# Three expert passes summed by TensorE alone, from rows gathered as 4 picks x 32 tokens, with 16 row buffers and two ring slots

## What is computed

```python
def peer_ffn(x, w_q, sub_keys, u, v):        # 8 heads, top 16: 128 picks a token
    q = (xt @ w_q).reshape(T, PEER_HEADS, 2, PEER_HALF)
    s = jnp.einsum('thcd,hcnd->thcn', q, sub_keys)
    s1, i1 = lax.top_k(s[:, :, 0], K); s2, i2 = lax.top_k(s[:, :, 1], K)
    ...                                       # best 16 of the 256 sums -> expert_idx, softmax -> gates
    ub = jnp.take(u, eb, axis=0)              # rows of 1024 numbers, 4 KB
    act = gelu(einsum('thkd,td->thk', ub, xb))
    vb = jnp.take(v, eb, axis=0)
    return einsum('thk,thkd->td', gb * act, vb)
```

## Time and profile before

| | |
|---|---|
| median of 3 runs | 2260.46 us (2255.74 to 2270.28) |
| span of the profiled execution | 2259.6 us (the profile records no time outside it) |
| busy in the span | PE 1527.2, DVE 1450.5, POOL 985.0, ACT 323.1 us |
| DMA | 760.62 MB, mean 337 GB/s; of it 536.94 MB by gathers |
| first gather issued | 208.45 us |
| last v row used | 1937.91 us |

### The profile page before, as it was taken

How to read it: one execution, slowest core, us unless ns; L and a number is a source line. 1 busy time by engine, 2 the same in 40 slices (tenths; PEclk the granted TensorE clock), 3 DMA queues, 4 the chain that set the end, 5 groups by cost and what they waited for, 6 DMA issues and landing times. The chain is left out here.

```text
span 2259.6 us, 17114 instructions
## 1 busy us (share of the span) xinstructions
PE 1527.2 (68%) x5282; PEld 879.4 (39%) x5282; DVE 1450.5 (64%) x3168; ACT 323.1 (14%) x778; POOL 985.0 (44%) x1058
## 2 busy tenths in 40 slices
PE   8987600467656539776573897666576656899998
PEld 7446600222225225422341552235252232376453
DVE  1236898779587875678688468786978676444101
ACT  1220100011112111111120111111321000123111
POOL 0102466667665555566455456653446444000000
PEclk9989855688867669987766899778767877899999
DMA  7436999999999999999999999999989999973672
GB/s 260 85 117 245 394 408 409 337 360 370 371 379 403 404 406 358 361 365 367 407 399 405 365 342 368 375 401 386 391 293 403 399 398 399 366 243 130 242 260 93
DMA packets 268005, 760.62 MB, mean 337 GB/s; under 512 B 21295, under 2 KB 46590, under 8 KB 267275
## 3 DMA queue, kind: packets, MB, share of 16 engines
q0 software_dynamic: 147456, 536.94, 61.8%
q1 hardware_dynamic: 120458, 222.60, 27.8%
HBM read 756.84 MB, written 2.62 MB: 336 GB/s over the span
## 5 line engine op out<-in xcount | busy, mean ns | idle before, releaser
L946 POOL DMA_INDIRECT ROWS<-in_peer_u,IDX x512 | 483.3, 944 | 455.5 <-DVE ROWS L991 266.9
L946 POOL DMA_INDIRECT ROWS<-in_peer_v,IDX x512 | 487.8, 953 | 357.2 <-PE bank L292 121.4
L991 DVE SCALAR_TENSOR_TENSOR ROWS<-ROWS,XP 128x1024 f32<-128x1024 f32 x512 | 602.3, 1215 | 23.7 <-issue 12.3
L995 DVE SCALAR_TENSOR_TENSOR XP<-ROWS,GATE,XP 128x1024 f32<-128x1024 f32 x316 | 405.8, 1284 | 155.9 <-DMA ROWS<-in_peer_v,IDX 133.7
L292 PE MATMUL bank<-ROWS,DG 128*128 128x512 f32 x774 | 380.0, 649 | 94.2 <-DMA ROWS<-in_peer_v,IDX 78.5
L292 PE MATMUL bank<-ring,XT 128*128 128x512 f32 (+6 forms) x912 | 392.7, 589 | 62.3 <-DMA ring<-in_ffn_w_up 32.0
L292 PEld LDWEIGHTS bank<-ring,XT 128*128 128x128 f32 x912 | 185.6, 214 | 249.9 <-issue 179.4
L292 PEld LDWEIGHTS bank<-ROWS,DG 128*128 128x128 f32 x774 | 157.5, 209 | 309.8 <-issue 201.8
L292 PE MATMUL bank<-XT,ring 128*128 128x128 f32 (+2 forms) x1504 | 209.4, 301 | 57.1 <-issue 27.4
L292 PEld LDWEIGHTS bank<-XT,ring 128*128 128x128 f32 (+1 forms) x1504 | 198.3, 204 | 71.8 <-issue 35.7
L307 PE MATMUL bank<-CN,X 128*128 128x128 f32 x128 | 27.1, 384 | 184.9 <-issue 90.7
(11 more groups left out here) (408 smaller groups left out, 1461.6 us busy)
## 6 DMA issues: line engine op xcount, KB each, us to landing
ring<-in_peer_w_q SPq DMA_DIRECT2D x16, 2048.0 KB
ring<-in_ple_w_gate SPq DMA_DIRECT2D x9, 2048.0 KB
...
ROWS<-in_peer_u,IDX POOLq DMA_INDIRECT x512
```

The lines of the kernel that those rows point to most:

```text
L946: G.indirect_dma_start(ROWBUF[slot(n, c)][:, :], None, tables[table], bass.IndirectOffsetOnAxis(IDX[:, tt, c:c + 1], axis=0)).then_inc(row ...
L991: V.scalar_tensor_tensor(row, row, 1.0, XP[:, :], ALU.mult, ALU.mult, accum_out=ACTV[:, tt, c:c + 1]).then_inc(row_used, 1)
L995: V.scalar_tensor_tensor(XP[:, :], row, gate, XP[:, :], ALU.mult, ALU.add).then_inc(row_used, 1)
```

## The change

1. **Passes 1, 3 and 5 wholly on TensorE.** `pe_turn_picks` and `dve_turn_picks` turn the table of indices (`IDXF` to `IDXV`), so that a gather brings 4 picks of 32 tokens, partition 32k + i being pick k of token i in the group. The bytes of a gather and their number stay. The gates are turned likewise (`pe_to_quads`, 32 matmuls of 16 columns) and DVE spreads them (`dve_spread`): four instructions of 1024 columns a pass, which make for each gather a stationary operand of 128 rows x 32 columns. PE multiplies a row buffer with it, 2 x 512 columns, and the result goes to 32 of the 128 output partitions: those of q = 0, 1, 2 or 3, by the gather's number in its group of 4. Gathers are taken in pairs: first columns 0 to 511 of both (into accA), then 512 to 1023 of both (accB), and one `pe_used` for the pair. The `DG` buffers and ACT's `act_share` are gone, and DVE has no row of these passes. `dve_sums` reads X and the banks after two rows of the next u pass.
2. **16 row buffers and two ring slots in passes 0 to 5.** The third slot's memory becomes row buffers 12 to 15. From pass 6 on these four are a ring slot again, and 12 row buffers are left. The early loads are placed by a table (`FIRST_SLOT`), some of them in row buffers.
3. **The query weights of layer 0 are loaded once** for both tiles: four loads of 2.10 MB less. Two of the four blocks lie in row buffers 8 to 11 and 12 to 15, so gathers 8 and 12 of pass 0 wait (`kept_read`) until ACT has copied tile 1's queries of those blocks, which are now made first (order 2, 3, 0, 1); the first gather waits for `out_w_read`.
4. DVE does 24 u rows of pass 0 at the end of layer 0's route, ahead of `dve_turn_picks`; the turned picks of later passes are made in `peer_done`.

Its core (lines left out stand as "..."):

```diff
-SLOTS = 12
+SLOTS = 16
 VECTORS = 13
-DIAGS = 4
+GROUP = 4
+QUAD = P // GROUP
...
-RING, SLOT = 3, 4096
+RING, SLOT = 2, 4096
+LATE = SLOTS * D // SLOT - 1
+NARROW = 6
 BANKS = 6
 MORE = SLOTS * D // SLOT
+KEPT_SLOT = {2: 5, 3: 2}
+FIRST_SLOT = {"a_gate": 0, "a_q": 1, "a_k": 3, "a_v0": 4, "a_v1": 0, "a_og0": 1, "a_og1": 3, "keys0": 0, "a_out0": 4, "a_out1": 3,
+              "peer_q0_0": 1, "peer_q0_1": 0, "peer_q0_2": KEPT_SLOT[2], "peer_q0_3": KEPT_SLOT[3]}
...
+            if key in FIRST_SLOT:
+                slot = FIRST_SLOT[key]
+            elif not fewer_rows:
+                slot = (n - len(FIRST_SLOT)) % RING
+            elif not last_gather:
+                slot = (n - fewer_rows[0]) % (RING + 1)
+            else:
+                slot = (n - last_gather[0] + RING + 1) % (RING + MORE)
+            slot_no.append(slot)
+            slot_use.append(slot_no[:n].count(slot))
...
-        enter_cols("peer_q01_", a["peer_w_q"][0], [0, 512, 1024, 1536, 2048])
...
+        fewer_rows.append(len(stream))
...
+                    if n == fewer_rows[0] + RING:
+                        sp.wait_ge(row_used, dve_used(NARROW - 1))
+                        sp.wait_ge(pe_used, tensor_used(NARROW - 1))
+                    elif last_gather[0] <= n < last_gather[0] + MORE - 1:
                         sp.wait_ge(row_used, dve_used(len(passes) - 1))
                         sp.wait_ge(pe_used, tensor_used(len(passes) - 1))
+                    elif before:
+                        sp.wait_ge(*released[before[-1]])
+                    elif n == place["peer_q0_3"]:
+                        sp.wait_ge(S("phase_end"), 3)
...
+        BY_PE = (1, 3, 5)
...
-            return n in SHARED and c % (2 * RUN) >= RUN
+            return n in BY_PE
...
+            if n < NARROW:
+                return (n * PICKS + c) % SLOTS
+            return ((n - NARROW) * PICKS + c) % (SLOTS - SLOT // D)
...
+            return (sum(len(pe_rows_of[m]) for m in range(n)) + (len(pe_rows_of[n]) if k is None else k) + 1) // 2
...
+                if n == 0 and c in (8, 12):
+                    G.wait_ge(S("kept_read"), c // 4 - 1)
+                picks = IDXV if n in BY_PE else IDX
                 G.indirect_dma_start(ROWBUF[slot(n, c)][:, :], None, tables[table],
-                                     bass.IndirectOffsetOnAxis(IDX[:, tt, c:c + 1], axis=0)).then_inc(row_in[slot(n, c)], 16)
+                                     bass.IndirectOffsetOnAxis(picks[:, tt, c:c + 1], axis=0)).then_inc(row_in[slot(n, c)], 16)
...
+                    if n == 0:
+                        pool.wait_ge(S("out_w_read"), 1)
+                    if n in BY_PE:
+                        pool.wait_ge(S("picks_turned"), n // 2 + 1)
...
+        def pe_to_quads(src, name):
+            m = src.shape[1] // GROUP
+            b = job(name)
+            if turn(name) > 1:
+                PE.wait_ge(bank_free(name), turn(name) - 1)
+            for k in range(GROUP):
+                for q in range(GROUP):
+                    last = mul(b[QUAD * k:QUAD * k + QUAD, q:GROUP * m:GROUP], ident[:, QUAD * q:QUAD * q + QUAD],
+                               src[:, k:GROUP * m:GROUP], True, True)
+            last.then_inc(bank_ready(name), 1)
...
+        def dve_turn_picks(l, tt):
+            V.wait_ge(bank_ready("turned"), turn("turned"))
+            V.tensor_copy(IDXV[:, tt, :], result("turned")[:, 0:PICKS]).then_inc(bank_free("turned"), 1)
+            V.wait_ge(bank_free("turned"), turn("turned"))
+            V.sem_inc(S("picks_turned"), 1)
...
+        def spread(tt, x):
+            part = Y[:, tt, :] if x == 2 else later["spread"][:, min(x, 2), :]
+            return part.rearrange("p (j t) -> p j t", t=QUAD)
+        def dve_spread(n, half):
+            tt, name = passes[n][1], f"gv{half}"
+            V.wait_ge(bank_ready(name), turn(name))
+            for x in (2 * half, 2 * half + 1):
+                gates = result(name)[:, QUAD * (x % 2):QUAD * (x % 2) + QUAD]
+                V.tensor_tensor(spread(tt, x), con("spread").unsqueeze(1).broadcast_to([P, QUAD, QUAD]),
+                                gates.unsqueeze(2).broadcast_to([P, QUAD, QUAD]), ALU.mult).then_inc(spread_ready, 1)
+            V.wait_ge(spread_ready, 4 * (n // 2) + 2 * half + 2)
+            V.sem_inc(bank_free(name), 1)
+        def pe_share(n, g0=0, g1=PICKS // GROUP):
+            accs, tt = (result("accA"), result("accB")), passes[n][1]
+            for g in range(g0, g1):
+                first, end = g == 0, g == PICKS // GROUP - 1
+                x, j = divmod(GROUP * g, QUAD)
+                PE.wait_ge(spread_ready, 4 * (n // 2) + x + 1)
+                weights = spread(tt, x)
+                for pair in ((0, 1), (2, 3)):
+                    for q in pair:
+                        PE.wait_ge(*arrived(n, GROUP * g + q))
+                    for q in pair:
+                        to, row = slice(QUAD * q, QUAD * q + QUAD), ROWBUF[slot(n, GROUP * g + q)]
+                        last = mul(accs[0][to, :], weights[:, j + q, :], row[:, 0:512], first, end)
+                    if end and 3 in pair:
+                        last.then_inc(bank_ready("accA"), 1)
+                    for q in pair:
+                        to, row = slice(QUAD * q, QUAD * q + QUAD), ROWBUF[slot(n, GROUP * g + q)]
+                        if end and q == GROUP - 1:
+                            held.clear()
+                            mul(accs[1][to, 0:256], weights[:, j + q, :], row[:, 512:768], False, True).then_inc(bank_ready("accB"), 1)
+                            last = mul(accs[1][to, 256:512], weights[:, j + q, :], row[:, 768:1024], False, True)
+                        else:
+                            last = mul(accs[1][to, :], weights[:, j + q, :], row[:, 512:1024], first, end)
+                    last.then_inc(pe_used, 1)
...
+            A.wait_ge(row_used, dve_used(n))
+            act_copy_x(n + 1)
...
+            if n not in BY_PE:
+                gather_rest()
+                V.scalar_tensor_tensor(Y[:, tt, :], X[:, tt, :], ALPHA, XP[:, :], ALU.mult, ALU.add).then_inc(S("sums_taken"), 1)
+                V.wait_ge(S("sums_taken"), 1)
                 return
+            V.wait_ge(*nth("x_copied", 2))
+            gather_begin(n + 1)
+            gather_some(2)
             V.wait_ge(pe_used, tensor_used(n))
             for i, name in enumerate(("accA", "accB")):
                 V.wait_ge(bank_ready(name), turn(name))
-                y = Y[:, tt, i * 512:(i + 1) * 512]
-                V.tensor_tensor(y, y, result(name)[:, :], ALU.add).then_inc(bank_free(name), 1)
+                s = slice(i * 512, (i + 1) * 512)
+                V.scalar_tensor_tensor(Y[:, tt, s], X[:, tt, s], ALPHA, result(name)[:, :], ALU.mult, ALU.add).then_inc(bank_free(name), 1)
+            gather_some(1)
...
+            to_pe = n + 1 in BY_PE
+            if to_pe:
+                @block.tensor
+                def _(pe):
+                    for i, half in enumerate(halves):
+                        pe.wait_ge(*nth("gate_done", i + 1))
+                        pe_to_quads(GATE[:, tt, half], f"gv{i}")
+                    pe_share_begin(n + 1)
+                    pe_share(n + 1, 0, 2)
...
+                if to_pe:
+                    gather_some(2)
+                    dve_spread(n + 1, 0)
...
-                        pe_share(beside, 6 * e, 6 * e + 6)
+                    if l == 1 and e > 0:
+                        pe_share(beside, 4 * e - 2, 4 * e + 2)
...
-                    for e in range(4):
-                        pe.wait_ge(*landed(f"peer_q{l}{tt}_{e}"))
-                        queries(slot_of(f"peer_q{l}{tt}_{e}"), tt, e)
-                        weight_read(f"peer_q{l}{tt}_{e}", f"q{e}{tt}")
+                    for e in (2, 3, 0, 1):
+                        queries(slot_of(f"peer_q{tag}_{e}"), tt, e)
+                        weight_read(f"peer_q{tag}_{e}", f"q{e}{tt}")
...
+                        A.sem_inc(S("out_w_read"), 1)
...
+                            A.sem_inc(S("kept_read"), 1)
...
+                if l == 0:
+                    gather_some(24)
+                    dve_turn_picks(0, 0)
```

125 lines of the change are left out of this document (53 added, 72 removed).

## The result

The changed kernel took **2327.5 us** (median of 4, 2325.8 to 2329.0) beside 2258.1 for the kernel before: ratio 1.030, interval 1.0272 to 1.0328. The forecast was 2207. But the verdict did not hold everywhere. On five later occasions, each on another chip of known number, the kernel before took 2264 once (chip 6) and 2193 to 2195 four times (chips 0, 12, 11, 4). On chip 12 the changed kernel took 2188, ratio 0.9972 (0.9955 to 0.9989). Two things stay open about these names. The number of the first chip is not on record, so it may be one of the others. And the two slow-issue occasions were the first two in time, and none of the five known chips was met twice: whether the kind belongs to a chip or to a time no run tells.

The account below looks back on a forecast made before the run. DMA engines were taken to bound the 1730 us middle, with v passes losing time to POOL's waits for PE. 2259.6 - 49.4 - 4 = 2206.2, with the median 0.9 above: 2207 us; range 2172 to 2262.

Parts of the forecast that it names:

- Why do they lose?: Passes 1, 3, 5: POOL has next to no reserve, so its waits for PE lose 62.4 us of DMA time.
- the 49.4 us: Passes 1, 3, 5: gain expected from part 1, 62.4 less 13 us of remaining losses; bounds 62 and 41.
- part 2, priced at nothing: Mixer in passes 2 and 4: two slots cost nothing until it is 40 us slower, since PE waited 41.91 us.
- Rival D: V passes as forecast, but first gathers, a mixer over 40 us late or late picks take it back: about 2231; chance 0.12.
- Part 1's price: V rows on PE: overlapping matmuls of different column groups make a row cost 0.87 us, against 1.75 at full clock.
- Rivals B and C: V rows on PE: B, 1.26 us a row, 2236 (0.08) or far slower (0.04); C, 1.75 us, 2412 us (0.16).
- a fall to half clock: PE in v passes: its clock may halve, making a row 1.75 us; the forecast took full clock.
- PE is then far from the bound: Passes 1, 3, 5: v rows need 111 us of PE a pass, 151 us in sum in passes of 202 and 207.
- Part 3, 4 us gained: Pass 0, query weights loaded once: 16 us of loads saved less 12 us of gather waits; bounds -5 and +12.
- Cover in passes 3 and 5: Query block of 16 us covered by 20 us of buffers; 5 us each still lost, bounds 0 and 9.
- Rival E: V passes: nothing changes, as lost DMA time has another cause (turned rows or loads between them): 2256; chance 0.04.
- The prediction's chance for slower (0.20): Whole kernel: chance of a slower result, made of C and B's far case.

Follow-up runs that it names:

- part 1 alone: Changed kernel with parts 2 and 3 undone, against the kernel before: 2281.4 us (1.0076) on chip 6, 2181.6 us (0.9945) on a quick chip.
- plain_index: Changed kernel with gathers of passes 1, 3 and 5 using the unturned index table, against the kernel before, chip 0: 2187.5 us (0.9964).

## Why the prediction was wrong

The forecast of 2207 missed 2327.5 by 120 us. By the pass table, 62 of them are the v passes (12.1 us longer in place of 49.4 shorter), 37 are passes 2 and 4, which were to stay as they are, and 23 are pass 0 (19 longer in place of 4 shorter); what is left nearly cancels.

- **The first step that failed is the answer to "Why do they lose?", and with it the 49.4 us.** That the v passes of the kernel before were short of DMA rate is right. I put the 62.4 us down to POOL's waits for TensorE, and those to the order of turns and to query blocks longer than 12 buffers. On chip 12 the same kernel with the same turns and the same 12 buffers runs these passes at 405, 401 and 402 GB/s. POOL's waits for TensorE in passes 0 to 5 are 72.2 us there against 121.4 on the first chip, so over half of them can stand in a run that DMA fills. Rows that said so stood in the trace that I had: a query block of 5.30 us for its first 46 matmuls and 16 us in all, 7.5 more than on chip 12. I took those for the block's own time. Late starts of TensorE explain passes 3 and 5 in part (14 and 12 us, where these passes are 19 us longer than on chip 12) and pass 1 less (6 of 18). What else the first chip loses there, and what makes instructions late, stays open.
- **The second is part 2, priced at nothing: 40 to 49 us on chip 6.** I took TensorE's 41.91 us at the mixer's end for slack of the whole kernel. It covers only TensorE: VectorE waits inside the mixer for TensorE and has u rows behind those waits. Rival D had put its condition the same way (a mixer late by more than its 40 us), and that did not happen: in pass 2 of the changed kernel TensorE still waited 16.68 and 20.76 us for gates behind the mixer, and the pass was 19 us longer all the same. Passes 2 and 4 are 21 us of part 2's cost. For the 12 us in pass 0 no reason is shown beyond the creeping there. On a quick chip, nothing was right.
- **Part 1's price: the sign was right, the size too high.** 0.87 us was forecast, 0.51 measured on queued rows and 0.96 for a lone pair. Rivals B and C, a row of 1.26 or 1.75 us because of loads or missing overlap, are both refuted, and so is a fall to half clock through a whole v pass (the granted clock was 0.97 in pass 1 on chip 12, and on the first chip 0.90 there and 0.81 and 0.78 in passes 3 and 5). The Trainium skill's rule in "TensorE: Matmul & The Clock Gate", Part 3 (Packing small matmuls), that a weight load overlaps running matmuls only when its row group differs, does not hold here: with all rows in each, loads lay under the matmuls.
- **"PE is then far from the bound": right for the time that its matmuls need, wrong for what it delivered.** In the second half of pass 1 on the first chip gathers went out at 1.43 us a row, waiting for TensorE. I had not counted that the change brings 5282 matmuls to 6338, but part 1 alone, which has them all, costs 0.8% on chip 6 and not 3.
- **Part 3, 4 us gained: 3 to 10 lost on the slow-issue kind and 5 on the quick one** (0.9972 against 0.9951), none of it clear of the intervals. The gathers' waits came to 18.7 us and not 12, on both kinds.
- **Cover in passes 3 and 5:** 16 x 1.28 = 20 us did not cover what crept (7 waits of POOL, 42.7 us in pass 3).
- **Rivals.** Rival E named another cause than waits for buffers, with 0.04, but its candidates were turned rows, which `plain_index` refutes on a quick chip, or loads, and its outcome was 2256. The prediction's chance for slower (0.20) belonged to kernels in which a row costs too much. That 2327.5 came out slower was for neither reason.
- **On a quick chip** the prediction comes near (2188 on chip 12, with 2193.5 for the kernel before), and that is luck: nothing came back in GB/s in the v passes, part 3 cost where it was to gain, and part 1 alone gained 0.55% there for a reason that no run isolates.
